# RWKV's 32-row low-rank products alternate between two row groups in one visit, and both halves of the 96-row product share one

## What is computed

```python
def rwkv7_time_mix(z, mu, w0, w2, a0, a2, g2, k_k, k_a, r_k, ln_w, ln_b):
    z = z + (token_shift(z) - z) * mu
    r, k, v, xw, xa, xg = jnp.split(z, RWKV_SPLITS, axis=-1)   # 512, 512, 512, 32, 32, 96 wide
    logw = -jax.nn.softplus(-(w0 + jnp.tanh(xw) @ w2)) - 0.5
    decay = jnp.exp(-jnp.exp(logw.astype(f32)))
    a = jax.nn.sigmoid(a0 + xa @ a2)
    g = jax.nn.sigmoid(xg) @ g2
    ...
    kk = heads(k * k_k)
    k = k * (1.0 + (a - 1.0) * k_a)
    ...
    _, y = lax.scan(step, state0, seq)
```

## Time and profile before

| | |
|---|---|
| median of 3 runs | 940.78 us (940.57 to 940.81) |
| span of the profiled execution | 938.8 us |
| profiled execution's own time | its span and about 2.0 us around it (940.8) |
| PE busy | 917.2 us, 98% |
| PE weight loads | 771.0 us, 82% |
| DVE busy | 598.4 us, 64% |
| ACT busy | 446.8 us, 48% |
| granted TensorE clock | 1.000 |

### The profile page before, as it was taken

How to read it: one execution, slowest core, us unless ns; L and a number is a source line. 1 busy time by engine, 2 the same in 40 slices (tenths; PEclk the granted TensorE clock), 3 DMA queues, 4 the chain that set the end, 5 groups by cost and what they waited for, 6 DMA issues and landing times.

```text
span 938.8 us, 15782 instructions
## 1 busy us (share of the span) xinstructions
PE 917.2 (98%) x6760; PEld 771.0 (82%) x6760; DVE 598.4 (64%) x952; ACT 446.8 (48%) x722; POOL 43.9 (5%) x60
## 2 busy tenths in 40 slices
PE   7999999999999999999999999999999999999997
PEld 5999887777889988888889988776778798888885
DVE  4668755764684566655765567877772456666773
ACT  4773344255542444445652446483531345455571
POOL 0010000100000000000000350000000000000000
PEclk9999999999999999999999999999999999999999
DMA  9544332222466766555356774343446556665531
GB/s 331 180 134 137 123 104 91 61 77 91 178 231 206 218 185 196 200 181 184 129 180 156 159 242 138 114 169 123 162 151 199 133 163 192 189 180 181 192 121 45
DMA packets 131205, 150.79 MB, mean 161 GB/s; under 512 B 11808, under 2 KB 102176, under 8 KB 131008
## 3 DMA queue, kind: packets, MB, share of 16 engines
q1 hardware_dynamic: 129920, 145.57, 49.7%
q10 hardware_dynamic: 1216, 4.23, 1.2%
HBM read 148.73 MB, written 1.05 MB: 160 GB/s over the span
## 4 chain that ended last, share of the span: by engine, by line
PE 89%; DVE 6%; ACT 2%; issue 2%; DMA 1%; POOL 0%; POOLq 0%; ACTq 0%
PE psum L825 11%; PE psum L714 9%; PE psum L716 9%; PE psum L715 8%; PE psum L826 6%; PE psum L777 6%; PE psum L797 4%; PE psum L798 4%; PE psum L806 4%; PE psum L720 3%; PE psum L873 3%; PE psum L883 2%; PE psum L874 2%; PE psum L828 2%; PE psum L1643 1%
## 5 line engine op out<-in xcount | busy, mean ns | idle before, releaser
L1746 ACT ACTIVATE parts<-low 128x1024 fp32r<-128x1024 f32 (+3 forms) x246 | 248.6, 1044 | 82.4 <-PE psum L716 60.5
L2574 DVE TENSOR_TENSOR parts<-low,parts 128x1024 fp32r<-128x1024 f32 (+3 forms) x150 | 181.3, 1235 | 22.9 <-ACT parts L1746 22.5
L714 PE MATMUL psum<-parts 128*128 128x512 f32 (+2 forms) x424 | 170.1, 401 | 1.0 <-DVE parts L2574 1.0
L716 PE MATMUL psum<-parts 128*128 128x512 f32 (+2 forms) x424 | 163.6, 386 | 0.0
L715 PE MATMUL psum<-parts 128*128 128x512 f32 (+2 forms) x424 | 163.4, 385 | 0.0
L825 PE MATMUL psum<-parts 128*128 128x512 f32 x434 | 155.6, 398 | 0.0
L1746 ACT ACTIVATE high<-psum 128x512 f32<-128x512 f32 (+4 forms) x102 | 55.8, 564 | 161.7 <-PE psum L828 73.1
L826 PE MATMUL psum<-parts 128*128 128x256 f32 x496 | 129.1, 281 | 0.0
L826 PEld LDWEIGHTS psum<-parts 128*128 128x128 f32 x496 | 93.6, 189 | 5.7
L714 PEld LDWEIGHTS psum<-parts 128*128 128x128 f32 x424 | 79.6, 188 | 21.2 <-issue 2.7
L825 PEld LDWEIGHTS psum<-parts 128*128 128x128 f32 x434 | 81.7, 188 | 16.9
(11 more groups left out here) (318 smaller groups left out, 1356.4 us busy)
## 6 DMA issues: line engine op xcount, KB each, us to landing
low<-in_w_in_dram SPq DMA_DIRECT2D x40, 1024.0 KB, 5.2
low<-in_w_ffn_in_dram SPq DMA_DIRECT2D x44, 512.0 KB, 5.2
low<-in_w_ff_in_dram SPq DMA_DIRECT2D x16, 1024.0 KB, 5.6
low<-in_w_ff_out_dram SPq DMA_DIRECT2D x16, 1024.0 KB, 4.9
low<-in_w_ffn_out_dram SPq DMA_DIRECT2D x11, 1024.0 KB, 5.0
low<-in_w_out_dram SPq DMA_DIRECT2D x8, 1024.0 KB, 5.2
low<-in_w_ple_gate_dram SPq DMA_DIRECT2D x4, 1024.0 KB, 4.9
low<-consts_dram ACTq DMA_DIRECT2D x1, 2142.0 KB, 9.1
```

The costliest lines, as they stand in the source:

```text
L714: mm(o, l[0], r[0], start, False)
L716: return mm(o, l[1], r[0], False, stop)
L1746: return e.activation(o, a, ACT.Copy)
L2574: tt(rslot3(n, nk, width)[:, r, 0:w], slot3(n, nk, width)[:, r, 0:w], st.hi3(j)[:, r, 0:w].bitcast(F32), ALU.subtract) \
```

## The change

- PE: the four visits of the products `w` and `a` become two. A visit takes two banks and four matmuls: for each of two blocks of features first `w` (partitions 0 to 31 of both operands) into one bank and then `a` (partitions 32 to 63) into the other. The two visits of `g` become one with four matmuls. No matmul is added or left out.
- ACT reads in the new order: `w` and `a` of one half, then of the other, then both halves of `g`. DVE's work around them is put into fewer turns, and POOL's generator counts 3 turns less.
- `order_1`: the first 18 letters are written out. The new visits come after m4, m7 and m11; the one of `n` after m14. From there on every visit comes one step later than before (before: s9 after m13, s13 after m19; now s6 after m14, s10 after m20), until the end, where both orders have used 92 steps.

```diff
--- before.py
+++ after.py
@@ -546,7 +546,7 @@
               "wo2": (A["w_out_2"][0], [P + 26152, P + 28200, P + 19968, P + 17920], m2Hi, m2Lo)}
 
         def order_1():
-            return itertools.chain("msmsm" * 12, "msmsmsm" * 5, "ms" * 35, "mssss", itertools.cycle("ms"))
+            return itertools.chain("msmmmsmmmsmmmmsmsm", "msmsm" * 8, "msmsmsm" * 5, "ms" * 35, "mssss", itertools.cycle("ms"))
 
 
 
@@ -1003,15 +1003,22 @@
                 yield
                 q.wait_ge(*rw_act.at("th"))
                 for h in range(2):
-                    product("w", h, lambda c: lo[0:32, 128 * c:128 * c + 128], lambda c: zm[0:32, 12, :], rw_act.at("w", h, 1))
-                    yield
-                for h in range(2):
-                    product("a", h, lambda c: lo[32:64, 128 * c:128 * c + 128], lambda c: zm[32:64, 12, :], rw_act.at("a", h, 1))
+                    bs = [next(rw_bank) for _ in range(2)]
+                    os_ = [bank(b) for b in bs]
+                    for j in range(2):
+                        c = 2 * h + j
+                        for n, name in enumerate(("w", "a")):
+                            r = slice(32 * n, 32 * n + 32)
+                            t = mm(os_[n][:, 256 * j:256 * j + 256], lo[r, 128 * c:128 * c + 128], zm[r, 12, :], True, True)
+                            if j == 1:
+                                t.then_inc(rw_pe.up(name, h), 1)
+                    for n, name in enumerate(("w", "a")):
+                        free[bs[n]] = [rw_act.at(name, h, 1)]
                     yield
                 q.wait_ge(*rw_act.at("sg"))
                 for h in range(2):
                     product("g", h, lambda c: lo[0:96, 512 + 128 * c:512 + 128 * c + 128], lambda c: zm[0:96, 13, :], rw_act.at("g", h))
-                    yield
+                yield
                 yield
                 b = next(rw_bank)
                 p = bank(b)
@@ -1940,19 +1947,19 @@
                 q.wait_ge(*z_dve.at(13))
                 act(zm[0:96, 13, :], zm[0:96, 13, :], ACT.Sigmoid).then_inc(rw_act.up("sg"), 1)
                 yield
-                for name, dst, bias in (("w", E4, "rwkv_w0"), ("a", A4, "rwkv_a0")):
-                    for h in range(2):
+                for h in range(2):
+                    for name, dst, bias in (("w", E4, "rwkv_w0"), ("a", A4, "rwkv_a0")):
                         p = bank(next(rw_bank))
                         q.wait_ge(*rw_pe.at(name, h))
                         for j in range(2):
                             act(dst[:, 512 * h + 256 * j:512 * h + 256 * j + 256], p[:, 256 * j:256 * j + 256], ACT.Sigmoid,
                                 bias=vec(bias, 2 * h + j)).then_inc(rw_act.up(name, h, j), 1)
-                        yield
+                    yield
                 for h in range(2):
                     p = bank(next(rw_bank))
                     q.wait_ge(*rw_pe.at("g", h))
                     copy(G4[:, 512 * h:512 * h + 512], p).then_inc(rw_act.up("g", h), 1)
-                    yield
+                yield
                 q.wait_ge(*rw_dve.at("kk"))
                 act(BON, KK, ACT.Square).then_inc(rw_act.up("k2"), 1)
                 q.wait_ge(*rw_dve.at("cc"))
@@ -2704,24 +2711,18 @@
 
             def rwkv():
                 yield
-                next(rw_bank)
-                yield
-                next(rw_bank)
-                yield
-                next(rw_bank)
+                next(rw_bank), next(rw_bank)
+                yield
+                next(rw_bank), next(rw_bank)
                 q.wait_ge(*rw_act.at("w", 1, 1))
                 q.wait_ge(*rw_pool.at("one"))
                 e.tensor_tensor_scan(CS, onez, E4, 0.0, ALU.mult, ALU.add).then_inc(rw_dve.up("cs"), 1)
                 yield
-                next(rw_bank)
-                yield
-                next(rw_bank)
+                next(rw_bank), next(rw_bank)
                 q.wait_ge(*rw_dve.at("cs"))
                 tt(v8(CSC), v8(CS), v8(CS)[:, :, 63:64].broadcast_to([128, 8, 128]), ALU.subtract).then_inc(rw_dve.up("cc"), 1)
                 q.wait_ge(*rw_dve.at("cc"))
                 tt(fct.unsqueeze(2), v42(CSC)[:, :, 0, 127:128], v42(CS)[:, :, 1, 63:64], ALU.add).then_inc(rw_dve.up("f"), 1)
-                yield
-                next(rw_bank)
                 for c in range(4, 8):
                     q.wait_ge(*z_dve.at(c))
                 tt(v4(KK), zk, bc(vec("rwkv_k_k", 0, 4), 256), ALU.mult).then_inc(rw_dve.up("kk"), 1)
@@ -3555,7 +3556,7 @@
                 q.wait_ge(*rw_pool.at("one0"))
                 e.memset(v8_of(onez), 0.0).then_inc(rw_pool.up("one"), 1)
                 yield
-                yield from steps(6)
+                yield from steps(3)
                 yield
                 q.wait_ge(*rw_act.at("g", 1))
                 e.memset(H0_f, 0.0).then_inc(rw_pool.up("h0"), 1)
```

## The result

The changed kernel took 943.44 us (median of 17 runs, 940.26 to 945.42), the kernel before, in turn with it, 940.57 us (17 runs, 940.23 to 940.99). The ratio is 1.0026, 95% interval 1.0019 to 1.0032: slower by 0.3%, which is small but clear of the interval, where 938.3 was forecast. The spread says as much as the median: 5.2 us after, 0.8 before. The 17 times stand in four heaps: 940.3 to 940.8 (3 runs), 941.9 to 942.6 (5), 943.4 to 943.9 (7), 945.2 to 945.4 (2), 1.4 to 1.7 us from heap to heap. The profiled execution, 945.2 us with a span of 943.3, is in the last.

A forecast was written before the change was run, and what follows sets the result against it. PE was taken as the bound, busy 917.2 us of a 938.8 us span. From 940.8 us, 2.46 came off for the merged w and a visits and 0 for waits, giving 938.3 us, range 937.1 to 940.3.

The forecast's parts named there:

- The products of w and a: Four visits merged into two of eight overlapping passes, 1.25 us each: 4.96 − 2.50 = 2.46 us saved on PE.
- the price without overlap: Rival for the merged w and a visits: 2.10 us each, only 0.76 us saved, 940.0 us; 12 in 100.
- The staggered rival: Merged w and a visits: row-group pairs start staggered, 0.21 us more per visit, 0.43 in all, 938.7 us; 5 in 100.
- The product of g: One merged visit of eight passes takes 1.72 us against 2 × 0.86; nothing saved (0.02 at most).
- m17's wait: PE reaches step m17, the first of 512 columns, earlier while ACT does not; it waits 0.5 us there.
- Scan, subtraction and `kk`: DVE's scan and the work behind it come later but ready some 2.7 us before m13 needs them: no cost.
- The visits that come one step later: From m57 on, beside attention: old waits go, new ones come, 5.2 us, or 5.7 with m17's, against 6.0; taken as even.
- the old 6.0 us: PE's waits from 90 to 245 us before the change, nearly all for masks, copies or softmax; all but 0.2 should go.
- new waits of 1.6, 2.4 and 0.9: X visits waiting for bank 4: behind the third scores 1.6 us, the fourth 2.4, six transposes 0.9.
- the 6.5 that the prediction had named as a sign of being wrong: PE's waits from 88 to 243 us, forecast near 5 us; wrong if above 6.5 or below 4.
- The sum: Whole kernel: 940.8 − 2.46 − 0 = 938.3 us, with the waits taken as even.
- The rival "bank 4": Bank 4's new waits (4.9 us) come on top of all the old ones: 943.7 us, slower; 6 in 100.

## Why the prediction was wrong

- **The products of w and a, 2.46 us: right.** 1.26 us for the visit; the price without overlap was right too (1.7 us more). The staggered rival is out. In the run with `w`, `w`, `a`, `a`, if the conclusion about it holds, a pass of `a` started ahead of passes of `w` that stand in front of it.
The Trainium skill (TensorE: Matmul & The Clock Gate, "The mechanism") has matmuls of different row groups start strictly in program order; by that, the run should have shown one pass in its first 0.1 us, and it shows two.
- **The product of g: right**, 1.73 for 1.72.
- **m17's wait: right**, 0.44 for 0.5. Scan, subtraction and `kk` cost nothing: right.
- **"The visits that come one step later": this step failed.** It said that all but 0.2 of the old 6.0 us should go, and they did; and it listed new waits of 1.6, 2.4 and 0.9, and they came as 1.76, 2.35 and 0.7. The list was short of two: 2.3 us for bank 4 at m67, which LR has written right before, and 0.7 for the last transposes. I had followed bank 4 behind the scores, and not in the step where the transposes follow LR. LR wrote that bank ahead of m67 in both kernels; what changed was how little PE and how much DVE had to do between. The waits came to 8.0 instead of 5.2, 2.8 more (7.3 of them from 88 to 243 us, above the 6.5 that the prediction had named as a sign of being wrong). The prediction had also rounded 5.7 against 6.0 to even, which is 0.3 less. 938.3 + 2.8 − 0.3 = 940.8 us: the upper end of the fastest heap.
- **The sum took every duration at full clock: the second half of the miss.** The trace of before has no clock drop and no wait over 1.1 us there (its only longer one, 5.5 us, is PE's for its first data, at the start of the span), so nothing in it priced one. I forecast a wait of 2.4 us and priced it at 2.4. From the fastest heap (940.3 to 940.8) to the median of 943.4 are 2.6 to 3.2 us: the median lies in the third heap, two losses of 1.4 to 1.7 us up.
- **The rival "bank 4" had the right number (943.7) by the wrong road.** It let the old waits stay, which all went, and it had no clock in it: that its number came near is luck.

Open: why a drop follows a wait of 2 us in one execution and not in the next, and which of several it follows.

## What to carry to other kernels

When an order shifts, list for each step not only which wait it has but what the releasing engine does between the two ends of it; a wait that is free in one order is 2.3 us in the next. A wait of about 2 us on a busy TensorE can cost more than its length: two of 1.0 us were 1.1 us cheaper here than one of 1.9. A median that moves with a spread that grows, in steps of one size, is a hint to look at the granted clock before anything else. Keep a gain apart from the shift it brings: merged and placed anew, the same edit gives 938.3 us in place of 943.4.

## What the runs showed of the hardware

- In the profiles, PE's first data and the program's last microseconds apart, there are 14 waits of PE of 1.76 to 2.83 us. Behind nine of them the granted clock fell to 0.50 (1.2 GHz), between the wait's last 0.1 us and 1.7 us after it, and behind five (1.76, 1.77, 1.77, 2.35 and 2.83 us) it did not. It stayed there for 3.4 us, once for 6.8 (the changed kernel's first), which costs 1.7 us and 3.4.
- In the seven kernels whose longest wait is 1.0 to 1.4 us no profile shows such a fall, and no run whose clock is on record has a mean below 0.998. Their spreads are 0.5 to 1.5 us, the widest in 22 runs of the kernel before.
- Two 32-row products written one behind the other, all of the first ahead of all of the second, had two passes at work from the visit's start when they were in different row groups (eight passes in 1.14 us); alternating but in one row group they had one (1.99 us).
